# Three transformer layers on one core: a norm's scale deferred behind squared-ReLU layers, earlier row maxima in the sparse heads, and a reordered opening and convolution

## Chip, core and metric

The kernel runs on one core of a Trainium2 chip. The metric is device time in microseconds for one execution. The engines are TensorE (PE in the profile, with PEld for its weight loads), VectorE (DVE), ScalarE (ACT), GpSimd (POOL) and SyncE (SP, which here only issues DMAs). Each engine runs its own instructions in order and waits on semaphores.

## What is computed

One sequence of 256 tokens with 1024 features, float32, passes through three layers. Cut to what matters:

```python
for i in range(2):                      # first_block
    h = rms_norm(x, g[0])
    m = parallel_conv_mla(h, ...) if i == 0 else conformer_conv(h, ...)
    x = x + rms_norm(m, g[1])
    h = rms_norm(x, g[2])
    x = x + rms_norm(square(relu(h @ w1)) @ w2, g[3])
# third layer: differential attention (4 heads) + sparse attention (8 heads), then a gated FFN
h = rms_norm(x, pre);  x = x + rms_norm(hybrid_mixer(h), post)
h = rms_norm(x, pre2); x = x + rms_norm((silu(h @ w_gate) * (h @ w_up)) @ w_down, post2)

def rms_norm(x, g): return x * rsqrt(mean(x * x) + 1e-6) * g
def conformer_conv(h):                  # layer 1's mixer
    a, b = split(h @ w_pw1 + b_pw1)
    u = depthwise_conv(a * sigmoid(b), w_dw) + b_dw       # 31 taps
    return silu(layer_norm(u)) @ w_pw2 + b_pw2
```

`parallel_conv_mla` (layer 0) projects h to gate_b, gate_c, xs and latents, computes gate_b * conv3(gate_c * xs), an 8-head attention with rotary parts, and multiplies both by w_out. In the sparse attention each of 8 heads has a selected and a windowed branch plus a branch over 15 compressed tokens; at 256 tokens the first two are causal over everything.

## The kernel before

The 256 tokens are two tiles (m = 0, 1) of 128 partitions. All products are made to float32 accuracy from two-part numbers: a matrix W is kept as w_hi (rounded) and w_lo (the rest), activations as act_hl with a high half and a low half, and a product is high times high, high times low and low times high. Weights stream in pieces of 128x2048 values (1 MB) through a ring of four slots (three in the last stage). For each piece SP issues the load into `raw` (`load`), waiting for `w_split` of the piece that had the slot; POOL (`hi`, L575, in loops L590 and L685) or ACT (`hi`, L1338) writes w_hi; DVE (`lo`, L704, in halves `lo_half`, L718) writes w_lo and counts `w_split`; PE uses them and counts `pe_piece`.

PE has two kinds of product: `tall` puts activations as the stationary side, 128 tokens by up to 512 columns, into banks ACC to ACC+3; `wide` puts weights as the stationary side and leaves a transposed result in banks UP to UP+3, whose columns T to 2T (the product with the activations' low half) ACT copies out before DVE adds them. `wide_by_tile` does the first two pieces of a stage tile by tile: 32 high products of tile 0, 16 low products of tile 0 (`low_part`), then `turn_m` (eight transposes of tile 1's normalized rows), 32 high products of tile 1, and the remaining low products. `keep_warm` issues bf16 products with no use for the result.

A transition (`boundary(s, last)`, s = 1 to 5) lies between two products: post-norm of the result, addition to x, pre-norm, transposes. For a tile: ACT squares the result (`post_square`, L1342), POOL takes rstd (`row_rsqrt`, two steps L608, L609), DVE multiplies by the gain (`post_gain`, L749) and adds to x (`post_add`, L770), ACT squares the new x (`x_square`, L1342), POOL takes rstd again, DVE writes nrm (`pre_tile`, L780), PE transposes (L1727), ACT writes the high part (`high_tile`, L1366), DVE the low part (`low_tile`, L789). s = 1 leads into layer 0's squared ReLU, 2 into the convolution layer, 3 into layer 1's squared ReLU, 4 into the third layer, 5 into the last FFN. The opening is the second half of this alone, on x as loaded.

The order on each engine is written out by hand. Around the change it is:

- Opening: SP loads x0, x1 and four pieces; ACT asks for the first gain and the identity; POOL takes both rstd and then copies pieces; DVE does `pre_tile(0)`, `pre_tile(1)`, `low_tile(0)`, `lo_until(1)` (both first pieces), `low_tile(1)`.
- Projection: three wide products (gate_b, gate_c, xs) in the same banks. ACT copies four banks' second halves into ctmp (`wide_half`, L1414), DVE adds four banks (`wide_sum`, L878), and PE may then overwrite them (`wide_read`).
- First attention: DVE alternates `head_weigh(h)` and `head_max(h+2)`, with the low part of gate_b and two `lo_half` between heads; ACT has exponentials, copies of transposed probabilities and, at head 3, one `hi`.
- Convolution: per block b of 256 channels, PE has `pw` (in two halves), `forward(b)` (a DFT), `inverse(b)`; DVE has `gated`, `filtered`, `lo`. Then `row_stats`, normalization (L1066), `turn_normed`, SiLU (ACT L1550, L1554, L1328; DVE L1074, L736) and pw2.
- Sparse heads, u = 4 to 11: PE `scores_of(u)`, DVE `row_max(u)` (L1152, L1153), ACT `exponentials(u)` (L1630, four calls), DVE `weigh(u)` (L1162, L1173, L1177), PE `turn_of(u)` (six transposes), ACT `probs_turned(u)` (L1643), and for every pair of heads `out_of_pair` on PE. On DVE the compressed branch (`compressed_shift`, `compressed_weigh`) and the norm of the differential heads (L1244 to L1251) lie between.

```python
for t in range(DH + 2, HEADS + 2):      # DVE, the sparse loop's head
    if t <= HEADS:
        weigh(t - 1)
    if t < HEADS:
        row_max(t)
```

## Time and profile before

| | us |
|---|---|
| median of 3 timed runs (lowest to highest) | 965.57 (963.13 to 968.69) |
| profiled execution, its own time | 964.97 |
| its span, first to last instruction | 963.2 |
| PE busy | 912.3 (95%) |
| DVE busy | 690.8 (72%) |
| POOL busy | 290.2 (30%) |
| ACT busy | 260.5 (27%) |
| DMA, mean | 167 GB/s |

In the rows below a timeline line gives the start and the duration in us, the engine, the line of the kernel, the operation, what is written and read, and, in brackets, how long the engine was idle before it and who released it. Lines of equal instructions in a row are merged; "x2" is their number. "PEclk" is the clock granted to TensorE as a share of full speed.

### The profile page before, as it was taken

The numbers are of one execution on the slowest core, as the hardware profiler recorded it, in microseconds if no ns is written. First come the engines' busy times: TensorE is split into PE (matmuls) and PEld (weight loads), VectorE is DVE, ScalarE is ACT, GpSimd is POOL, SyncE is SP. The second block draws the span as 40 slices with busy tenths as digits, with TensorE's granted clock in tenths as the row PEclk, the third lists the DMA queues.
The fourth block names the chain that finished last, engine by engine and source line by source line (L and its number), as shares of the span: only waits on it lengthen the run. The fifth ranks groups of instructions, "written<-read, shape, count | busy, mean of one in ns | idle before, by whom it ended". The sixth has DMA issues, their size and how long they took to land.

```text
span 963.2 us, 12984 instructions
## 1 busy us (share of the span) xinstructions
PE 912.3 (95%) x4940; PEld 765.9 (80%) x4940; DVE 690.8 (72%) x695; ACT 260.5 (27%) x514; POOL 290.2 (30%) x176
## 2 busy tenths in 40 slices
PE   4999899999999999899999999999987999999996
PEld 4987688888888688688888888788855888888885
DVE  5668768876777645659877677677767578676774
ACT  2437441111112500323111111255665221111112
POOL 5000024444445332123344442400000234333331
PEclk9999999999999999999999999999999999999999
DMA  8752326555566354315555555456400437656631
GB/s 295 258 198 92 131 88 219 183 208 205 188 254 206 111 175 150 112 45 197 196 181 209 206 215 181 147 180 214 153 1 20 156 128 223 213 178 186 206 131 44
DMA packets 82437, 160.89 MB, mean 167 GB/s; under 512 B 4942, under 2 KB 40633, under 8 KB 82400
## 3 DMA queue, kind: packets, MB, share of 16 engines
q1 hardware_dynamic: 82112, 159.78, 48.3%
q8 instruction: 26, 0.43, 0.2%
q10 hardware_dynamic: 288, 0.59, 0.2%
q14 instruction: 11, 0.09, 0.0%
HBM read 159.31 MB, written 1.05 MB: 166 GB/s over the span
## 4 chain that ended last, share of the span: by engine, by line
PE 80%; DVE 11%; ACT 4%; POOL 2%; issue 2%; DMA 1%; DVEq 0%; SPq 0%; POOLq 0%; ACTq 0%
PE ps L1723 78%; DVE w_lo L704 2%; PE ps L1727 2%; ACT arena L1342 2%; ACT arena L1630 1%; DVE x_res L770 1%; DVE nrm L780 1%; POOL st L609 1%; POOL st L608 1%; DMA x_res<-in_x 1%; DVE arena L1177 1%; DVE w_lo L718 0%; DVE act_hl L789 0%; DVE st L1153 0%; DVE nrm L749 0%
## 5 line engine op out<-in xcount | busy, mean ns | idle before, releaser
L704 DVE TENSOR_TENSOR w_lo<-raw,w_hi 128x2048 fp32r<-128x2048 f32 (+3 forms) x140 | 331.5, 2394 | 35.3 <-POOL w_hi L685 21.7
L1723 PE MATMUL ps<-act_hl,w_hi 128*128 128x512 f32 (+1 forms) x1088 | 243.9, 371 | 9.5 <-DVE act_hl L789 7.6
L1723 PEld LDWEIGHTS ps<-act_hl,w_hi 128*128 128x128 f32 x1088 | 185.6, 194 | 39.7 <-DVE act_hl L789 9.0
L1723 PE MATMUL ps<-w_hi,act_hl 128*128 128x512 f32 (+3 forms) x656 | 184.3, 381 | 6.6 <-DVE act_hl L736 2.4
L590 POOL TENSOR_SCALAR w_hi<-raw 128x2048 fp32r<-128x2048 f32 x56 | 137.9, 2463 | 169.6 <-PE ps L1723 169.6
L1723 PE MATMUL ps<-w_hi,hl 128*128 128x512 f32 (+2 forms) x680 | 186.3, 384 | 0.6 <-DVE w_lo L704 0.6
L1723 PEld LDWEIGHTS ps<-w_hi,hl 128*128 128x128 f32 (+1 forms) x680 | 125.7, 189 | 24.1 <-issue 0.8
L1723 PEld LDWEIGHTS ps<-w_hi,act_hl 128*128 128x128 f32 x656 | 118.6, 188 | 31.6 <-DVE act_hl L736 2.9
L1723 PEld LDWEIGHTS ps<-act_hl,w_lo 128*128 128x128 f32 x1024 | 135.9, 190 | 8.3 <-DVE w_lo L704 0.2
L1723 PE MATMUL ps<-act_hl,w_lo 128*128 128x256 f32 (+1 forms) x1024 | 139.2, 281 | 0.0
L575 POOL TENSOR_SCALAR w_hi<-raw 128x2048 fp32r<-128x2048 f32 (+3 forms) x28 | 56.6, 2026 | 173.2 <-PE ps L1723 129.3
L1723 PE MATMUL ps<-w_lo,hl 128*128 128x512 f32 (+1 forms) x356 | 108.1, 378 | 0.0
L1723 PE MATMUL ps<-w_lo,act_hl 128*128 128x512 f32 (+1 forms) x328 | 107.4, 378 | 0.0
L685 POOL TENSOR_SCALAR w_hi<-raw 128x2048 fp32r<-128x2048 f32 x27 | 55.4, 2053 | 97.2 <-PE ps L1723 93.0
L1723 PEld LDWEIGHTS ps<-w_lo,hl 128*128 128x128 f32 (+1 forms) x356 | 65.3, 184 | 12.7
L1338 ACT ACTIVATE w_hi<-raw 128x2048 fp32r<-128x2048 f32 (+2 forms) x34 | 63.8, 1875 | 35.8 <-PE ps L1723 15.1
L998 DVE TENSOR_TENSOR hl<-arena,hl 128x512 fp32r<-128x512 f32 x28 | 53.7, 1923 | 25.3 <-ACT hl L1507 25.3
L1723 PEld LDWEIGHTS ps<-w_lo,act_hl 128*128 128x128 f32 x328 | 59.8, 188 | 11.0
L1499 ACT ACTIVATE arena<-ps 128x512 f32<-128x512 f32 x32 | 19.2, 598 | 143.4 <-PE ps L1723 143.4
L990 DVE TENSOR_TENSOR arena<-ps,arena 128x512 f32<-128x512 f32 x32 | 22.1, 690 | 43.7 <-ACT arena L1499 43.7
L1507 ACT ACTIVATE hl<-arena 128x512 fp32r<-128x512 f32 x28 | 17.8, 635 | 119.6 <-PE ps L1723 116.5
L1723 PE MATMUL ps<-arena 128*64 128x256 f32 (+6 forms) x288 | 43.2, 357 | 1.1 <-DVE arena L1043 0.9
(185 smaller groups left out, 709.2 us busy)
## 6 DMA issues: line engine op xcount, KB each, us to landing
raw<-in_mlp_w SPq DMA_DIRECT2D x64, 1024.0 KB, 5.2
raw<-in_w_gate SPq DMA_DIRECT2D x22, 512.0 KB, 4.0
raw<-in_w_up SPq DMA_DIRECT2D x22, 512.0 KB, 4.9
raw<-in_w_down SPq DMA_DIRECT2D x11, 1024.0 KB, 4.9
raw<-in_odd_w_pw SPq DMA_DIRECT2D x16, 512.0 KB, 4.9
raw<-in_w_in SPq DMA_DIRECT2D x8, 1024.0 KB, 5.4
raw<-in_even_w_in SPq DMA_DIRECT2D x6, 1024.0 KB, 8.1
raw<-in_even_w_out SPq DMA_DIRECT2D x4, 1024.0 KB, 6.0
```

The source lines that it names most:

```text
L575: gp.tensor_scalar(w_hi[slot_of(n)][:, 0:w], raw[slot_of(n)][:, 0:w], 1.0, 0.0, ALU.mult, ALU.add).then_inc(S("w_hi"), 1)
L590: gp.tensor_scalar(w_hi[slot_of(n)][:, :], raw[slot_of(n)][:, :], 1.0, 0.0, ALU.mult, ALU.add).then_inc(S("w_hi"), 1)
L685: gp.tensor_scalar(w_hi[slot_of(q)][:, :], raw[slot_of(q)][:, :], 1.0, 0.0, ALU.mult, ALU.add).then_inc(S("w_hi"), 1)
L704: tt(w_lo[slot_of(n)][:, 0:w], raw[slot_of(n)][:, 0:w], w_hi[slot_of(n)][:, 0:w].bitcast(F32), ALU.subtract).then_inc(S("w_split"), 1)
L990: link(tt(htmp[:, c, :], ps[:, UP + 2 * j:UP + 2 * j + 2, 0:T], htmp[:, c, :], ALU.add))
L998: tt(dst[:, c, T:2 * T], hb[:, c, :], dst[:, c, 0:T].bitcast(F32), ALU.subtract)\
L1338: f(w_hi[slot_of(n)][:, 0:w], raw[slot_of(n)][:, 0:w], ACT.Copy).then_inc(S("w_hi"), 1)
L1342: f(junk[:, m, at:at + src.shape[1]], src, ACT.Square, scale=1.0 / D ** 0.5, accum_out=total)\
L1499: f(htmp[:, 2 * j:2 * j + 2, :], ps[:, UP + 2 * j:UP + 2 * j + 2, T:2 * T], ACT.Copy)\
L1507: f(dst[:, 2 * j:2 * j + 2, 0:T], hb[:, 2 * j:2 * j + 2, :], ACT.Copy).then_inc(S("hid_hi"), 1)
L1723: return pe.matmul(o, l, r, start=start, stop=stop, skip_group_check=True)
L1727: return pe.transpose(o, src, ident[0:src.shape[0], 0:src.shape[0]])
```

## The change

Four things, on the same products with the same operands.

1. In transitions 1 and 3 (`SCALE_LATER`) the pre-norm does not wait for the rstd of the new x. `post_add_pre` multiplies by whatever rs_pre holds, c, from the norm before. Since the squared-ReLU layer is homogeneous of degree two, its result comes out (c/r)^2 times too large, r being the right scale, and the post-norm behind it removes any factor except in its eps. POOL's `next_eps` computes the eps that makes it exact, EPS * (c*c*(mean x^2 + EPS))^2, for use in transition s + 1. ACT writes tile 1's high part before it squares x. On PE, `wide_by_tile` has tile 1's transposes ahead of tile 0's low products (`turn_late=False`), here and in the opening.
2. Sparse heads: PE issues the scores one head further ahead and DVE takes the maximum of the next head before it weighs the current one.
3. Opening: loads in the order x0, piece 0, x1, piece 1; the first gain is asked for when x0 has landed; DVE has `low_tile(0)` and the low part of piece 0 before tile 1's norm.
4. Smaller orders: projection copies and sums in halves; first attention with the gate product earlier and weight work behind the heads; w_out's piece 0 with its w_lo products last; `inverse` one block behind; layer norm written by halves; SiLU's high part before the next tanh; `lo_half` before `pre_tile(1)` in transitions 2 and 5; w_lo of the last piece before the last SiLU; four `keep_warm` products after tile 1's transposes in transitions 4 and 5. TILE_STEP = (4, 4) names the grouping of the copies and leaves it as it was.

```diff
@@ SP @@
                 for m in range(M):
                     sp.dma_start(x[:, m, :], a["x"][0, m * P:(m + 1) * P, :]).then_inc(S(f"x_in{m}"), 16)
-                for n in range(4):
+                    load(m)
+                for n in range(2, 4):
                     load(n)
@@ POOL @@
+                def next_eps(m):
+                    squares[0] += 2
+                    gp.wait_ge(S("ssq"), squares[0])
+                    h, c = ssx[:, 2 * m:2 * m + 1], rs_pre[:, m:m + 1]
+                    me.link(gp.tensor_scalar(h, h, ssx[:, 2 * m + 1:2 * m + 2], EPS, ALU.add, ALU.add))
+                    me.link(gp.tensor_tensor(h, h, c, ALU.mult))
+                    me.link(gp.tensor_tensor(h, h, c, ALU.mult))
+                    me.link(gp.tensor_scalar(eps_next[:, m:m + 1], h, h, EPS, ALU.mult, ALU.mult))
...
                 row_rsqrt(rs_pre, ssx, 0)
+                hi_until(0)
                 row_rsqrt(rs_pre, ssx, 1)
@@ DVE @@
+                def post_add_pre(s, m, g):
+                    next_rstd()
+                    ssqs[0] += 4
...
+                    for i, h in enumerate(half):
+                        stt(x[:, m, h], nrm[:, m, h], rs_post[:, m:m + 1], x[:, m, h], ALU.mult, ALU.add)\
+                            .then_inc(S("x_new"), 1)
+                        dve.wait_ge(S("x_new"), 4 * (s - 1) + 2 * m + i + 1)
+                        stt(nrm[:, m, h], x[:, m, h], rs_pre[:, m:m + 1], gain[g % 4][:, h], ALU.mult, ALU.mult)\
+                            .then_inc(S("normed"), 1)
...
                 pre_tile(0, 0)
+                low_tile(0, ACC)
+                lo_until(0)
                 pre_tile(1, 0)
-                low_tile(0, ACC)
                 lo_until(1)
                 low_tile(1, ACC)
...
                 row_max(DH)
                 compressed_kv()
+                row_max(DH + 1)
                 weigh(DH)
-                row_max(DH + 1)
                 compressed_shift()
-                compressed_weigh()
                 for t in range(DH + 2, HEADS + 2):
-                    if t <= HEADS:
+                    if t < HEADS and t != DH + 3:
+                        row_max(t)
+                    if t <= HEADS and t != DH + 3:
                         weigh(t - 1)
-                    if t < HEADS:
-                        row_max(t)
                     if t == DH + 2:
+                        compressed_weigh()
+                        row_max(DH + 3)
+                        weigh(DH + 2)
...
-                lo_until(N_PIECES - 2)
+                lo_until(N_PIECES - 1)
                 silu_gate(FF_BLOCKS - 1)
                 ff_lo(FF_BLOCKS - 1, act_hl)
-                lo_until(N_PIECES)
@@ ACT @@
+                small(cst[:, 0:P], a["shape_constants"][:, 0:P], "cst_in")
+                act.wait_ge(S("x_in0"), 16)
                 small(gain[0][:, :], a["sandwich_gains"][0, 0, :].partition_broadcast(P), "gain0")
-                small(cst[:, 0:P], a["shape_constants"][:, 0:P], "cst_in")
...
-                    if h == 3:
-                        hi(c + 10)
...
                 pair_out(2, "pv", 4, 6)
+                hi(c + 10)
...
                     if k % 2:
+                        if k > 1:
+                            silu_high(k // 2 - 1)
                         act.wait_ge(S("z"), k + 1)
@@ PE @@
-                        if m == 1:
+                        if m == 1 and turn_late:
                             turn_m(turn_bank, 1)
+                            keep_warm(turn_bank, 4)
...
                         if m == 0:
+                            if not turn_late:
+                                turn_m(turn_bank, 1)
                             arrived(n)
                             low_part(n, slice(0, P), range(4))
...
-                    inverse(b)
+                    if b:
+                        inverse(b - 1)
+                inverse(3)
...
+                scores_of(DH + 2)
                 turn_of(DH)
                 for t in range(DH + 2, DH + NH + 1):
-                    if t < DH + NH:
-                        scores_of(t)
+                    if t + 1 < DH + NH:
+                        scores_of(t + 1)
```

## Rows read from the trace of the kernel before

**Rows 1.** The page, part 1: busy time, share and instructions of each engine.

```profile
PE 912.3 (95%) x4940; PEld 765.9 (80%) x4940; DVE 690.8 (72%) x695; ACT 260.5 (27%) x514; POOL 290.2 (30%) x176
```

**Rows 2.** Windows: length, busy us of each engine, PEclk, DMA share, GB/s.

```profile
0.00:27.00 27.00, 13.52 (x87) 12.91 (x88) 13.51 (x10) 6.23 (x13) 14.25 (x13) 1.00 0.87 306
...
84.00:110.00 26.00, 21.62 (x131) 14.82 (x130) 22.57 (x49) 19.72 (x53) 0.00 (x0) 1.00 0.13 41
...
138.00:152.00 14.00, 12.14 (x87) 11.31 (x87) 10.75 (x10) 5.99 (x6) 2.99 (x4) 0.88 0.48 174
152.00:315.00 163.00, 163.00 (x823) 139.01 (x823) 127.28 (x79) 22.73 (x42) 76.21 (x33) 1.00 0.58 205
...
388.00:404.00 16.00, 12.39 (x62) 8.52 (x61) 10.75 (x16) 5.49 (x11) 1.57 (x4) 1.00 0.41 131
...
431.00:443.00 12.00, 10.14 (x82) 9.31 (x81) 10.76 (x10) 5.91 (x6) 0.65 (x2) 1.00 0.44 155
...
688.00:742.00 54.00, 42.78 (x351) 31.11 (x351) 39.80 (x111) 36.55 (x115) 1.95 (x2) 0.97 0.09 30
```

**Rows 3.** DMA issues in 0 to 40 us: queue, size, us to landing.

```profile
gain<-in_sandwich_gains ACTq DMA_DIRECT2D x1, 512.0 KB, 5.6
```

**Rows 4.** Timeline of the opening.

```profile
10.69 1.89 POOL L575 TENSOR_SCALAR w_hi<-raw 128x2048 fp32r<-128x2048 f32 x1
10.74 3.04 DVE L780 SCALAR_TENSOR_TENSOR nrm<-x_res,st,gain 128x512 f32<-128x512 f32 x2 [0.77 <-POOL st L609]
...
14.44 6.13 PE L1723 MATMUL ps<-act_hl,w_hi 128*128 128x256 f32 x32 [3.04 <-DVE act_hl L789]
14.91 6.64 DVE L704 TENSOR_TENSOR w_lo<-raw,w_hi 128x2048 fp32r<-128x2048 f32 x2
...
15.78 7.52 POOL L575 TENSOR_SCALAR w_hi<-raw 128x2016 fp32r<-128x2016 f32 x2 [0.23 <-DMA raw<-in_even_w_in]
...
24.19 4.09 PE L1723 MATMUL ps<-act_hl,w_hi 128*128 128x256 f32 x32 [0.98 <-DVE act_hl L789]
```

**Rows 5.** Timeline of tile 1 in transition 1, and the same products in transition 3.

```profile
135.79 1.41 DVE L770 SCALAR_TENSOR_TENSOR x_res<-nrm,st,x_res 128x512 f32<-128x512 f32 x2 [0.42 <-POOL st L609]
...
139.04 1.42 DVE L780 SCALAR_TENSOR_TENSOR nrm<-x_res,st,gain 128x512 f32<-128x512 f32 x2 [1.83 <-POOL st L609]
...
142.37 5.42 PE L1723 MATMUL ps<-act_hl,w_hi 128*128 128x256 f32 x32 [1.20 <-DVE act_hl L789]
...
434.79 4.10 PE L1723 MATMUL ps<-act_hl,w_hi 128*128 128x256 f32 x32 [1.20 <-DVE act_hl L789]
```

**Rows 6.** Timeline, first products of the third projection.

```profile
60.64 2.12 PE L1723 MATMUL ps<-act_hl,w_hi 128*128 128x512 f32 x8 [1.28 <-DVE arena L878]
```

**Rows 7.** Timeline of the first attention: ACT's weight copy, and w_out's first products.

```profile
96.50 1.92 ACT L1338 ACTIVATE w_hi<-raw 128x2048 fp32r<-128x2048 f32 x1
...
109.38 0.72 PE L1723 MATMUL ps<-w_hi,act_hl 128*128 128x512 f32 x2 [0.69 <-ACT arena L1460]
```

**Rows 8.** Timeline, end of the convolution: last inverse, first products of pw2.

```profile
390.53 3.72 PE L1723 MATMUL ps<-arena 128*128 128x256 f32 x16 [0.95 <-DVE arena L1043]
...
403.05 0.74 PE L1723 MATMUL ps<-w_hi,act_hl 128*128 128x512 f32 x2 [2.44 <-DVE act_hl L736]
```

**Rows 9.** Timeline of the sparse heads, and w_out_2's first products.

```profile
712.69 1.54 PE L1727 MATMUL ps<-cst,arena 128*128 128x128 f32 x6 [2.77 <-DVE arena L1177]
...
732.45 0.37 ACT L1630 ACTIVATE arena<-ps,st 128x128 f32<-128x128 f32 x1 [1.72 <-DVE st L1153]
...
734.61 1.01 DVE L1177 TENSOR_SCALAR arena<-arena,st 128x128 f32<-128x128 f32 x4
...
736.58 0.37 ACT L1630 ACTIVATE arena<-ps,st 128x128 f32<-128x128 f32 x1 [1.44 <-DVE st L1153]
...
741.33 0.73 PE L1723 MATMUL ps<-w_hi,act_hl 128*128 128x512 f32 x2 [0.65 <-DVE act_hl L734]
```

**Rows 10.** Timeline, the last piece's first products.

```profile
950.94 0.70 PE L1723 MATMUL ps<-w_hi,act_hl 128*128 128x512 f32 x2 [0.96 <-DVE w_lo L704]
```

More of the change, by code:

```diff
@@ L623, in boundary @@
                         bias_low(0, bias_pw1)
-                    row_rsqrt(rs_post, ssh, 0)
-                    all_normed = 4 + 4 * s + (2 if s >= 3 else 0)
-                    row_rsqrt(rs_pre, ssx, 0)
+                    eps = [eps_next[:, m:m + 1] if s - 1 in SCALE_LATER else EPS for m in range(M)]
+                    row_rsqrt(rs_post, ssh, 0, eps[0])
+                    all_normed = 4 + 4 * s + (4 if s >= 3 else 0)
+                    if s in SCALE_LATER:
+                        next_eps(0)
+                    else:
+                        row_rsqrt(rs_pre, ssx, 0)
                     gp.wait_ge(S("normed"), all_normed - 2)
@@ L1380, in boundary @@
                         x_square(1, h)
-                    high_tile(1, TURN_BANK[s])
+                    if s not in SCALE_LATER:
+                        high_tile(1, TURN_BANK[s])
                     if s != 4:
@@ L1771, in wide, with tall @@
                     ins.then_inc(S("pe_piece"), 1)
-                def tall(n, bank, lhs, lhs_k0, first, last, k, cols, turn_=0, per=0, tiles=range(M), free=True, half=None, apart=2, split=512):
-                    arrived(n, turn_, per)
+                def tall(n, bank, lhs, lhs_k0, first, last, k, cols, turn_=0, per=0, tiles=range(M), free=True, half=None, apart=2, split=512, low_last=False):
+                    if low_last:
+                        pe.wait_ge(S("w_hi"), n + 1)
+                    else:
+                        arrived(n, turn_, per)
```

205 lines of the change are left out of this document (117 added, 88 removed).

## Prediction

> **What bounds the kernel now.** TensorE. It is busy 912.3 of 963.2 us [rows 1], so I read the profile in this order: the page for that share, a table of windows for where the missing 51 us lie, the list of who waits for whom for the releasers, and then the timeline around each hole. In the table the reader is to see that the long stages have no hole at all (163.00 busy of 163 in the first squared-ReLU block), while 13.5 us are missing in the opening, 4.4 in the first attention, 1.9 in each of the two transitions into a squared-ReLU layer, 3.6 at the end of the convolution, 11.2 in the sparse heads [rows 2]. What the change can give is in these holes, plus two stretches at half clock: the granted clock is 0.88 on average in 138 to 152 and 0.97 in 688 to 742, and 1.00 elsewhere in the table. Nothing else is priced: the change leaves every matrix product as it is.
>
> The profiled execution took 964.97 us with a span of 963.2; the median of the three timed runs is 965.57. The sum is made against 964.97, and I carry it over unchanged, since the 0.6 us between them is less than the spread of the runs.
>
> **Opening (+1.5 us).** The loads go x0, w0, x1, w1; the first gain is asked for on ACT's queue only once x0 has landed. Before, that gain took 5.6 us from issue to landing [rows 3] while x0 and x1 shared the engines. Issued at about 4.9 (x0 now travels nearly alone; before, both were under way from 0.7) and given a somewhat better rate than in the ramp, it lands near 9.6, and the first norm cannot start before. Bounds: 8.7 if it needs 3.8 us, 11.7 if x0 comes no earlier than now and the 5.6 stand. Meanwhile POOL copies w0 as soon as it is there, 1.89 us [rows 4]. The trace shows what happens when DVE's norm meets such a copy: the pair of multiplications takes 3.04 us at 10.74, against 1.42 with POOL idle [rows 4, 5]. Two DVE subtractions of w_lo take 6.64 instead of 4.6, and the two POOL copies beside them 7.52 instead of 3.8: the engines take turns, one instruction each [rows 4]. So the order in which they ask counts. Followed: copy w0 to 10.5, first half norm 11.2, transposes, ACT, low part, first real product at 13.7 instead of 14.44. Then alternately copy w1 to 15.2, low part of w0 to 17.5, copy w2 to 19.3, norm of tile 1 first half to 20.0, copy w3 to 21.9, second half to 22.6, low part of w1 to 24.9, low part of tile 1 to 25.6. The second tile's products then start at 25.7, where they start at 24.19 now [rows 4]. The order by which x1's norm stood ahead of the first low part is what the change gives up. Bounds: -2.0 if the turns fall so that DVE is never refused, +3 if the gain lands at 11.7 and the idle keeps the clock low.
>
> The Trainium skill, in "SBUF — State Buffer", section on who interferes with whom, says that a DVE instruction with two SBUF inputs and a GpSimd instruction that reads SBUF lock each other out for the whole instruction. The durations in [rows 4] agree; without the rule, and with the durations just split, one would book the opening as a gain of 2 us. The Trainium skill, in "DMA: Bandwidth & Descriptors", section on queues and rings, has the DMA engines serve the queues in turn, packet by packet; by it the gain gets half the rate and lands near 9.6. No row of before shows ACT's queue against a full SP queue.
>
> **Projection halves (-0.9).** The product after gate_c waits 1.28 us for one ACT copy and one DVE addition over four banks [rows 6]. Split in two, each half costs some 0.6 and 0.7 instead of 1.0 and 1.2, and PE needs only the first. Bounds 0 and -1.3.
>
> **First attention (-1.3).** ACT's copy of the last w_out piece, 1.92 us, stands between two heads [rows 7] and goes behind them; so do 1.2 us of gate low part and 2.4 of w_lo on DVE. Walking the eight heads by engine order (PE about 1.1 for scores, 0.6 for transposes, 1.1 per pair for values; ACT 0.95 and 0.6; DVE 0.7 and 0.8) PE becomes the fuller one but still waits for the last pairs; w_out starts at 108.1 instead of 109.38 [rows 7]. The work taken out is late next: w_lo of w_out's pieces. Piece 0 now runs its high parts first (16 products of 0.23, 3.6 us), and the low part is written before they end. The bound is the whole hole, -4.4; the other 0.
>
> **Transition into layer 0's squared ReLU (-2.5).** Now: post-norm's rstd of tile 1 at 135.79, x written, squares on ACT, two POOL steps, pre-norm at 139.04 after 1.83 idle, transposes, products at 142.37 after another 1.20 [rows 5]. The change multiplies by the scale left over from the norm before, at once: four DVE instructions from 135.79 end at 138.7, so the transposes end at 139.3 (after some 0.5 of new waiting for the second half), the sixteen low products of tile 0, which stood before them, now fill the copies' time (1.9 us), and the products start at 141.2: -1.2. The 32 products took 5.42 us at half clock here and 4.10 in the same place of the other layer [rows 5]; without the long wait I expect 4.1: -1.3. Its chance is less than certain, since the other layer has the same wait at full clock. The squares and next_eps move behind; POOL has nothing else until the next copy, and what they feed is a whole layer away. The correction itself costs eight tiny POOL instructions per layer.
>
> **The same in layer 1 (-1.2),** by the same steps: products at 434.79 after 1.20 idle [rows 5] start at 433.6. Bounds for either: 0 and -1.9.
>
> **Convolution (-2.0).** The last inverse transform waits 0.95 us for the filter [rows 8]; with the previous inverse behind the last forward one, that is covered, and row statistics fit in before it ends. Normalizing by halves brings the transposes forward by 1.2, but ten and four warming products stand before them, so only 0.4 arrives. SiLU's high part ahead of the next tanh saves another 0.6 of the 2.44 us wait [rows 8]. Bounds -0.9 and -3.4.
>
> **Sparse heads (-3.2).** Between one head's exponentials and the next lie 4.13 us (732.45 to 736.58), in which ACT works 1.6 and then waits while DVE weighs (1.4) and only then takes the maximum (1.0) [rows 9]. With scores one head ahead and the maximum first, the exponentials no longer wait for the weighing; late next is PE, 3.3 us a head (scores 1.3, transposes 0.9, half a pair 1.1). In the first four heads DVE also has the compressed branch and the norm of the differential heads, about 1.2 us per head, and ACT still has its 1.9 us weight copies in between. Walked by order of the queues, exponentials of the seventh head and later start 1 to 4 us earlier and w_out_2 starts at 738.1 instead of 741.33 [rows 9]. This includes the half clock that followed the 2.77 us wait [rows 9]. Bounds: 0 (a wait for the compressed branch takes the place) and -8, what is left of the 11.2 us hole and the low clock if only the waits ahead of the head loop stay [rows 2].
>
> **The end (-0.9).** The last low part, ahead of the last SiLU, fills DVE's idle and removes a 0.96 us wait [rows 10]. The copy it needs is there before. **Warming products** (four of 0.22) added where tile 1's transposes are done lie inside waits of about 1 us: 0, at worst +0.3 at each of two places.
>
> Sum: 1.5 - 0.9 - 1.3 - 2.5 - 1.2 - 2.0 - 3.2 - 0.9 = -10.5, so 954.5 us.
>
> **Rivals.** (a) The opening gains 2.0: 951.0. For it: the total work on the two engines is unchanged. Against: the 3.04 and 7.52 us. (b) The sparse heads gain nothing, because the DVE extras and ACT's weight copies still set the pace: 957.7. For it: DVE is the busiest beside PE there. (c) Clock: other waits draw a low stretch; each costs about 1.3 us, and before had two. With three in after, 4.0 worse than booked: 958.5. (d) Slower: the gain's load starves. If ACT's queue gets nothing while SP's is full, the gain lands with SP's first lull at about 22 us, and the second tile's products start 12 us after it, 34: the opening costs 9.8 and the total is 962.8. If it lands only behind the three gains that SP asks for next, about 30, the cost is 17.8 and the total 970.8. The loss outweighs the gain from a landing of 24.6 on. Against it: the gain of before landed in 5.6 us beside two loads of SP. (e) The deferred scale does not remove the wait, because the second half of the pre-norm arrives as late: 957 to 958.
>
> **How the numbers follow.** Forecast 0.52 (951 to 957), (a) 0.15, (b) 0.12, (c) 0.08, (e) 0.07, (d) 0.04 at 962.8 and 0.02 at 970.8. Measurement tells about 0.5% (4.8 us) from no change. Up to 960.7 is faster: all but (d) and a small tail of (c) and (e), 0.89; within 0.5% 0.08; slower 0.03. The range 947 to 960 reaches from (a) with a fuller attention and sparse gain to (c).
>
> **What would show it.** Right: windows over 84 to 110 with 1 us less idle; products after the two transitions behind a wait under 0.3 us, with the squares on ACT after the transposed copies; exponentials under 3.5 us apart; no wait for w_lo at the end; in the opening a DVE norm stretched beside a POOL copy. Wrong: a first product before 13 us and the second tile's before 23, a wait for the maximum as long as before, or a half-clock stretch in a long stage. My largest doubts are the opening's sign and the sparse size.

## The result, and the profile after

| | before | after |
|---|---|---|
| median of the timed runs, us | 965.68 (963.13 to 968.69) | 955.73 (954.66 to 956.50) |
| ratio, 95% interval | | 0.990 (0.987 to 0.993) |
| profiled execution: time and span, us | 964.97, 963.2 | 956.50, 954.4 |
| TensorE busy, us | 912.3 | 914.3 |

The change is 1.0% faster; forecast were 954.5 us and a range of 947 to 960. TensorE is still the bound, and its busy time has even grown, though its products are the same but for eight warming ones.
```profile
PE 914.3 (96%) x4948; PEld 767.9 (80%) x4948; DVE 691.4 (72%) x700; ACT 259.9 (27%) x517; POOL 299.2 (31%) x184
```

Windows over the same stages as in [rows 2], each shifted by what the kernel had gained by then (columns: window, length, busy us of each engine with instructions, granted clock, DMA share, GB/s):

```profile
0.00:27.00 27.00, 12.74 (x77) 11.84 (x78) 12.47 (x10) 6.35 (x13) 11.19 (x13) 1.00 0.87 306
84.00:109.00 25.00, 21.53 (x133) 15.34 (x131) 20.14 (x47) 18.18 (x53) 0.00 (x0) 1.00 0.00 1
135.00:149.00 14.00, 13.07 (x105) 12.43 (x105) 12.72 (x14) 7.86 (x11) 8.56 (x6) 1.00 0.40 149
320.00:333.00 13.00, 11.76 (x36) 7.51 (x35) 8.67 (x8) 6.76 (x6) 3.76 (x3) 0.74 0.49 153
385.00:401.00 16.00, 14.53 (x74) 11.04 (x73) 12.18 (x18) 4.57 (x10) 1.57 (x4) 1.00 0.42 131
427.00:439.00 12.00, 11.07 (x92) 10.54 (x91) 10.79 (x11) 7.60 (x11) 6.81 (x5) 1.00 0.43 144
684.00:735.00 51.00, 43.27 (x352) 31.43 (x353) 39.97 (x110) 36.09 (x115) 1.86 (x2) 0.97 0.08 31
```

The reader is to see two things. The holes have shrunk where the change works: 25.00 - 21.53 = 3.5 us are missing in the attention (4.4 before), 0.9 in either transition into a squared-ReLU layer (1.9 before), 1.5 at the end of the convolution (3.6), 7.7 in the sparse heads (11.2). In the opening the hole is 14.3 (13.5). And a window that [rows 2] did not need to show, the transition out of the first squared-ReLU layer, now runs at a mean clock of 0.74: 13 x 0.26 x 2 = 6.8 us of it at half clock. The lengths of low stretches below are worked out from windows in the same way.

For the sum I cut both traces at the same products. The cut M1 is the start of the second tile's products in the opening, M2 of w_out's, M3 the first tile's transposes into the transition behind the first squared-ReLU layer, M4 the first products of pw2, M5 and M6 two products at 608 and 697, M7 w_out_2's first, M8 one at 787. Each is a row of the timeline. Transitions 1 to 3 are those into the first squared-ReLU layer, out of it into the convolution layer, and into the second squared-ReLU layer. Times in us:

| stretch | before | after | difference | forecast | what changes in it |
|---|---|---|---|---|---|
| start to M1 | 24.19 | 25.49 | +1.30 | +1.5 | opening |
| M1 to M2 | 85.19 | 82.83 | -2.36 | -2.2 | projection halves, first attention |
| M2 to M3 | 207.35 | 204.77 | -2.58 | -2.5 | transition 1 |
| M3 to M4 | 86.32 | 87.20 | +0.88 | -2.0 | transition 2, convolution |
| M4 to M5 | 209.39 | 207.78 | -1.61 | -1.2 | transition 3 |
| M5 to M6 | 89.27 | 89.34 | +0.07 | 0 | |
| M6 to M7 | 39.62 | 36.47 | -3.15 | -3.2 | sparse heads |
| M7 to M8 | 53.42 | 53.29 | -0.13 | 0 | |
| M8 to the end | 168.45 | 167.23 | -1.22 | -0.9 | low part of the last piece |
| span | 963.2 | 954.4 | -8.8 | -10.5 | |

Eight stretches out of nine are within 0.5 us of their terms. The one that is not is M3 to M4, by 2.9 us, and the experiments begin there. (The medians differ by 9.9, the two profiled spans by 8.8; the runs of after alone spread over 1.8.)

The opening (timeline; columns: start, duration, engine, line, operation, idle before and its releaser), and the gain's row among the DMA issues (the last number is us from issue to landing):

```profile
8.92 1.90 POOL L585 TENSOR_SCALAR w_hi<-raw 128x2048 fp32r<-128x2048 f32 x1
...
12.07 1.42 DVE L808 SCALAR_TENSOR_TENSOR nrm<-x_res,st,gain 128x512 f32<-128x512 f32 x2 [12.07 <-DMA gain<-in_sandwich_gains]
...
13.11 2.14 POOL L585 TENSOR_SCALAR w_hi<-raw 128x2048 fp32r<-128x2048 f32 x1 [1.24 <-DMA raw<-in_even_w_in]
...
15.56 6.24 PE L1776 MATMUL ps<-act_hl,w_hi 128*128 128x256 f32 x32 [0.65 <-DVE act_hl L831]
15.58 1.89 POOL L585 TENSOR_SCALAR w_hi<-raw 128x2016 fp32r<-128x2016 f32 x1 [0.34 <-DMA raw<-in_even_w_in]
...
16.19 3.42 DVE L732 TENSOR_TENSOR w_lo<-raw,w_hi 128x2048 fp32r<-128x2048 f32 x1
18.10 3.25 POOL L585 TENSOR_SCALAR w_hi<-raw 128x2016 fp32r<-128x2016 f32 x1 [0.63 <-DMA raw<-in_even_w_in]
...
19.53 3.01 DVE L808 SCALAR_TENSOR_TENSOR nrm<-x_res,st,gain 128x512 f32<-128x512 f32 x2
...
25.49 4.06 PE L1776 MATMUL ps<-act_hl,w_hi 128*128 128x256 f32 x32 [0.50 <-DVE act_hl L831]
```

```profile
gain<-in_sandwich_gains ACTq DMA_DIRECT2D x1, 512.0 KB, 7.2
```

The first norm starts 2.5 us later than forecast and runs free of POOL's copy (1.42 for the pair), since that copy was over by then; the second tile's norm takes 3.01 beside a later copy (18.10), as the pair did in [rows 4].

Both transitions into a squared-ReLU layer, second tile (timeline):

```profile
134.46 0.75 DVE L818 SCALAR_TENSOR_TENSOR x_res<-nrm,st,x_res 128x512 f32<-128x512 f32 x1 [0.41 <-POOL st L619]
...
135.25 0.75 DVE L821 SCALAR_TENSOR_TENSOR nrm<-x_res,st,gain 128x512 f32<-128x512 f32 x1
...
137.51 0.66 PE L1780 MATMUL ps<-cst,nrm 128*128 128x128 f32 x4 [0.63 <-DVE nrm L821]
...
139.74 4.04 PE L1776 MATMUL ps<-act_hl,w_hi 128*128 128x256 f32 x32
...
142.04 2.16 POOL L628 TENSOR_TENSOR st<-st 128x1 f32<-128x1 f32 x1
...
428.16 0.65 PE L1780 MATMUL ps<-cst,nrm 128*128 128x128 f32 x4 [0.63 <-DVE nrm L821]
```

The pre-norm starts 0.79 us behind the start of the x update, where it stood 3.25 behind in [rows 5]. The 32 products start without a wait and take 4.04 instead of 5.42. The four transposes of the second half wait 0.63, in both layers.

The sparse heads (timeline): two exponentials of the last heads, and the waits around them.

```profile
719.40 0.93 PE L1776 MATMUL ps<-arena 64*128 64x128 f32 x8 [1.65 <-ACT arena L1683]
...
721.71 2.41 PE L1776 MATMUL ps<-arena 128*64 128x256 f32 x16
...
725.67 0.36 ACT L1683 ACTIVATE arena<-ps,st 128x128 f32<-128x128 f32 x1
...
728.21 0.41 ACT L1683 ACTIVATE arena<-ps,st 128x128 f32<-128x128 f32 x1
...
733.88 0.72 PE L1776 MATMUL ps<-w_hi,act_hl 128*128 128x512 f32 x2 [1.15 <-DVE act_hl L762]
```

The exponentials of the last four heads (from 717.64, 720.18, 725.67 and 728.21) come in pairs, 2.5 us apart within a pair and 5.5 between the pairs, where [rows 9] has 4.13; those of the first four are 3.6, 6.2 and 4.1 apart. So the last three gaps together are 10.6 us against 12.5 before. The longest wait is 1.65 instead of 2.77. The sixteen products at 721.71, most of them at half clock, take 2.41 us; the same sixteen at 728.62 take 1.47.

### The profile page after: what moved, and what is told of

Read it like the earlier page. It is cut to its first block, busy times and chain, and to the rows that moved or that the text cites. A ratio compares the mean times of both kernels' runs of the same rounds, so it can differ in the third digit from the quotient of the medians.

```text
span 954.4 us, 13013 instructions
## 1 busy us (share of the span) xinstructions
PE 914.3 (96%) x4948; PEld 767.9 (80%) x4948; DVE 691.4 (72%) x700; ACT 259.9 (27%) x517; POOL 299.2 (31%) x184
## 4 chain that ended last, share of the span: by engine, by line
PE 81%; DVE 10%; ACT 4%; issue 2%; POOL 2%; DMA 1%; DVEq 0%; POOLq 0%; ACTq 0%
PE ps L1776 79%; DVE w_lo L732 3%; PE ps L1780 2%; ACT arena L1390 1%; POOL st L618 1%; DVE x_res L798 1%; DMA gain<-in_sandwich_gains 1%; POOL st L619 1%; DVE nrm L808 1%; ACT w_hi L1386 1%; ACT arena L1683 0%; DMA x_res<-in_x 0%; DVE nrm L777 0%; DVE nrm L821 0%; POOL w_hi L585 0%
## 5 line engine op out<-in xcount | busy, mean ns | idle before, releaser
L585 POOL TENSOR_SCALAR w_hi<-raw 128x2048 fp32r<-128x2048 f32 (+3 forms) x28 | 54.4, 1944 | 170.0 <-PE ps L1776 138.1
```

Source lines behind the costliest of these rows:

```text
L585: gp.tensor_scalar(w_hi[slot_of(n)][:, 0:w], raw[slot_of(n)][:, 0:w], 1.0, 0.0, ALU.mult, ALU.add).then_inc(S("w_hi"), 1)
```

## The experiments

All of them are edits of the changed kernel. "Undone" means the lines of before, with one exception, said at e3_no_defer. Their medians are of four runs; since low-clock stretches come and go from trace to trace, the verdicts rest on the cuts M1 to M8, not on the medians.

### e1_warm_t2: what took the 2.9 us between M3 and M4

```
                     if m == 1:
+                        keep_warm(ACC, 5)
                         turn_m(ACC, 1)
                         pe.wait_ge(S("dft_in"), 16 * 16)
                         filter_of(0)
+                        keep_warm(ACC, 3)
```

> The changed kernel with eight warming products more at the transition out of the first squared-ReLU layer: five ahead of the second tile's transposes, where TensorE waits 1.23 us in the changed kernel (322.02), and three behind the filter's products. Theory: that wait, 0.29 us longer than the 0.94 at the same place of the kernel before, is what cost the clock (granted 0.62 over 325 to 333, where the sixteen products took 6.27 us against 3.93 before). With the wait filled the clock stays at 1.00, the sixteen products take about 3.9 us, and the kernel takes 955.7 - 3.4 + 0.3 = 952.6 us. Rival: the clock falls for what lies longer before (the whole stage has run faster) or falls later instead; then the time is 955.7 to 956.2, with the low stretch there or in the next stage.

Measured: 953.13 us (952.51 to 955.28), ratio 0.990 (0.989 to 0.992), span 950.4. The same two windows of after and of this kernel:

```profile
320.00:325.00 5.00, 3.76 (x15) 1.93 (x14) 3.37 (x6) 2.22 (x3) 1.01 (x2) 0.93 0.00 0
325.00:332.00 7.00, 7.00 (x18) 4.75 (x17) 5.30 (x3) 4.54 (x4) 2.21 (x1) 0.56 0.75 232
```

```profile
320.00:325.00 5.00, 4.86 (x22) 2.53 (x21) 3.37 (x6) 2.15 (x5) 1.01 (x2) 1.00 0.00 0
325.00:332.00 7.00, 7.00 (x31) 5.17 (x30) 5.67 (x4) 4.92 (x4) 1.83 (x1) 1.00 0.54 166
```

In 325 to 332 TensorE is busy all the time in both, but gets through 18 matmuls in the one and 31, three of them warming ones, in the other. With the wait filled the clock stays up, and M3 to M4 takes 84.53 instead of 87.20: 2.7 us. The low stretch is what took the time, as the theory has it. What I had not expected is that the one in the sparse heads went too (M6 to M7 34.88 instead of 36.47), though nothing was changed there.

Why the wait is longer than before can be read from the second tile's rows of this transition, in before (first line) and in after:

```profile
323.57 0.30 POOL L608 TENSOR_SCALAR st<-st 128x1 f32<-128x1 f32 x1 [2.37 <-ACT arena L1342]
```

```profile
319.08 1.22 DVE L746 TENSOR_TENSOR w_lo<-raw,w_hi 128x1024 fp32r<-128x1024 f32 x1
...
320.02 0.45 POOL L618 TENSOR_SCALAR st<-st 128x1 f32<-128x1 f32 x1 [2.37 <-ACT arena L1390]
```

The change itself put the half low part (`lo_half`) ahead of the second tile's pre-norm here, and POOL's step beside it takes 0.45 instead of 0.30. From the x update to the pre-norm pass 3.46 us (317.75 to 321.21) instead of 3.25; the remaining 0.08 of the 0.29 lies ahead of the x update. That the length of the wait decides is not shown. The six traces with this wait unfilled fit it, though: 0.94 and 1.14 us with no low stretch (before, e3_no_defer), 1.21 to 1.24 with one (after, e2_open_old, e4_sparse_old, e11_warm_sparse), each in one trace.

### e2_open_old: the opening undone

Loads in the order x0, x1, w0 to w3; the gain asked for ahead of everything on ACT's queue; x1's norm ahead of the first low parts; the second tile's transposes late.

> The changed kernel with the opening of the kernel before: loads x0, x1 ahead of the four weight pieces, the gain asked for at once, x1's norm ahead of the first low parts on POOL and DVE, the second tile's transposes behind the first tile's low products. Theory: the second tile's products start at 24.2 again instead of 25.5, the time falls by 1.3 to 954.4, if the low-clock stretch at the transition out of the first squared-ReLU layer stays; 951.0 if it goes. Rival (the opening of the change is a gain that shows only later, because DVE and POOL have then done more of the work): the product behind gate_c, 36 us later, starts as late as or later than in the changed kernel (60.95), and the time is 955.7 or more.

Measured: 955.20 us (954.62 to 955.63), span 953.3, 1.1 less than after. The two rows that answer to those of after:

```profile
10.80 3.05 DVE L806 SCALAR_TENSOR_TENSOR nrm<-x_res,st,gain 128x512 f32<-128x512 f32 x2 [0.78 <-POOL st L618]
...
24.46 4.06 PE L1772 MATMUL ps<-act_hl,w_hi 128*128 128x256 f32 x32 [1.07 <-DVE act_hl L829]
```

The second tile's products start at 24.46; with the opening of the change they start between 25.30 and 26.00 in the eight traces that have it unchanged, with the old one at 24.19, 24.46 and 24.70 in three (before, this run, e9_warm_open_old). M1 to M2 stays at 82.83, so nothing is given back later: the opening of the change costs 0.6 to 1.8 us, 1.0 in this pair. The rival falls.

### e3_no_defer: the deferred scale undone

```
-        SCALE_LATER = (1, 3)
+        SCALE_LATER = ()
```

> The changed kernel without the deferred scale: in all transitions the second tile's pre-norm waits for its own row sums (four warming products stand behind its transposes). Theory: the second tile's products start 1.2 us later at both transitions, and the 32 of the first take 5.4 us at the lower clock again or 4.1 with the warming products; 955.7 + 2.4 + (0 to 1.3) = 958.1 to 959.4, or 3.4 less if the low stretch at the next transition goes. Rival: the wait that the deferral removes is hidden elsewhere (the added second-half wait of 0.63 us, low parts of the weights late): 956.5 at most, with the w_lo pieces of the next products as the late ones.

Measured: 955.61 us (955.50 to 957.21), span 953.9: no slower than after. In one thing this kernel is not the one before: in transitions 1 and 3 it has the half low part ahead of the second tile's pre-norm, and four warming products behind the transposes. By the total the rival would win. By the cuts it does not: M2 to M3 is 205.87 (+1.10) and M4 to M5 209.58 (+1.80), so taking the deferral out costs 2.9 us, more than my 2.4; and M3 to M4 is 83.92 (-3.28), because no low stretch came at the second transition. Transition 1 in this kernel:

```profile
138.90 1.32 PE L1780 MATMUL ps<-cst,nrm 128*128 128x128 f32 x8 [0.57 <-DVE nrm L808]
...
140.05 1.03 PE L1776 MATMUL ps<-mask_neg,mask_id 128*128 128x512 bf16 x4
...
141.06 4.07 PE L1776 MATMUL ps<-act_hl,w_hi 128*128 128x256 f32 x32
```

The 32 products take 4.07 us here too. So the 1.3 us of half clock that before pays in this place [rows 5] does not hang on the deferral: with about the old wait, partly filled by four warming products, it is gone as well. Of the 1.80 in transition 3, 0.7 comes ahead of the second tile's pre-norm: its x is updated 25.50 us after M4 instead of 24.82, behind 0.79 us of waiting for POOL instead of 0.41.

### e4_sparse_old: the sparse heads undone

The weights of a head again come ahead of the next head's maxima, and the scores are one head ahead only.

> The changed kernel with the sparse heads in the order of the kernel before: weights of a head ahead of the next head's maxima, scores one head ahead only. Theory: 3.2 us more, 958.9, with the exponentials of the last heads 4.1 us apart again where they are 2.5 to 5.5 apart in pairs now, and the last wait ahead of w_out_2's products as before. Rival: the gain of the sparse stage came from elsewhere (work of the stages before done earlier by DVE and ACT): then under 1 us more, 955.7 to 956.7.

Measured: 957.19 us (956.16 to 958.12), span 955.8, 1.4 more than after; between theory and rival. Waits of TensorE in this kernel:

```profile
708.06 0.88 PE L1778 MATMUL ps<-cst,arena 128*128 128x128 f32 x6 [2.77 <-DVE arena L1223]
...
735.38 0.73 PE L1774 MATMUL ps<-w_hi,act_hl 128*128 128x512 f32 x2 [0.65 <-DVE act_hl L762]
```

The wait of 2.77 is back exactly as in [rows 9], but the six transposes behind it take 0.88 us and not 1.54: this run drew no low stretch in the sparse heads (it did at transition 2). Its M6 to M7 is 38.30. Against e1_warm_t2, the run of the new order without a stretch (34.88), the order is worth 3.4 us; before (39.62) against after (36.47), both with one, 3.2. The theory holds at equal clock, and my sentence that the 3.2 "includes the half clock that followed the 2.77 us wait" falls: after had a stretch as well, further on in the stage (2.41 instead of 1.47 us at 721.71).

### e5_attn_old, e6_conv_old, e7_halves_end_old: three more parts undone

These three start from e1_warm_t2, so that no stretch at transition 2 blurs them. e5 puts ACT's copy and DVE's low parts of w_out back among the heads; e6 restores `inverse(b)` behind `forward(b)`, normalization by tile and tanh ahead of the SiLU copy; e7 restores four-bank copies and sums in the projection and the last low part behind the last SiLU.

> The changed kernel with the warming of e1_warm_t2 (953.1 us, no low-clock stretch), and the first attention's tail in the order of the kernel before: ACT's copy of the last output-weight piece between two heads, gate and low parts among the heads on DVE, the first piece's products in one pass. Theory: the output products start 1.37 us later than in e1_warm_t2 (108.72), at 110.1; 954.5 us if no clock stretch is drawn, 956.0 to 957.9 with one. Rival (w_lo of those pieces, late next, had taken part of it back, or the attention's gain came from the projection halves ahead of it): under 0.5 us later.

> The changed kernel with the warming of e1_warm_t2, and the convolution in the order of the kernel before (inverse transform right behind its own block's forward transform, normalization by tile, tanh ahead of the SiLU high part). My sum booked 2.0 us for it; the two traces with their low stretch taken off show nearer 2.5. Theory: 953.1 + 2.5 = 955.6 us, with a wait of about 0.95 ahead of the last inverse transform and 2.4 ahead of the products behind it (403.05 in the kernel before), without a low stretch. Rival: one of the three edits does nothing and the stage loses only the 1.2 us by which that last wait shrank: 954.3.

> The changed kernel with the warming of e1_warm_t2, and both small edits undone, far apart from each other: the projection's copies and sums over four banks in one piece (start), and the last low part behind the last SiLU (end). Theory: the product after gate_c waits 1.28 us again instead of 0.33 (0.95 more), and the products of the last piece wait 0.96 again: 953.1 + 1.9 = 955.0 us. Rival: the wait of 0.96 at the end was the order's own and costs nothing of the span, as the last products wait for the down-projection's hidden rows anyway: 954.1.

Measured: 956.09, 957.35 and 957.34 us; spans 953.3, 954.2 and 955.7. One row, two rows and two rows of their timelines, in this order:

```profile
109.61 0.73 PE L1777 MATMUL ps<-w_hi,act_hl 128*128 128x512 f32 x2 [0.69 <-ACT arena L1514]
```

```profile
387.61 3.72 PE L1779 MATMUL ps<-arena 128*128 128x256 f32 x16 [0.95 <-DVE arena L1092]
...
400.13 0.74 PE L1779 MATMUL ps<-w_hi,act_hl 128*128 128x512 f32 x2 [2.44 <-DVE act_hl L764]
```

```profile
62.43 2.12 PE L1777 MATMUL ps<-act_hl,w_hi 128*128 128x512 f32 x8 [1.28 <-DVE arena L929]
...
943.46 0.70 PE L1777 MATMUL ps<-w_hi,act_hl 128*128 128x512 f32 x2 [0.96 <-DVE w_lo L732]
```

Against e1_warm_t2, M1 to M2 grows by 1.31 in e5 (attention) and by 1.02 in e7 (halves), M3 to M4 by 2.66 in e6, M8 to the end by 1.25 in e7. The waits of [rows 6, 8, 10] come back to the hundredth. The forecasts for those parts were 1.3, 0.9, 2.0 and 0.9, and the rivals of all three kernels fall. Their medians are 1.6 to 2.3 us above what was expected, by the low-clock stretches that each of them drew in the sparse heads: M6 to M7 is 36.45, 36.46 and, with a stretch of 6.8 us, 37.81, where e1_warm_t2 has 34.88 by the same instructions.

### e8_gain_now and e10_open_mixed: what sets the second tile's start

Both have the warming products of e1_warm_t2, and on ACT's queue:

```
+                small(gain[0][:, :], a["sandwich_gains"][0, 0, :].partition_broadcast(P), "gain0")
                 small(cst[:, 0:P], a["shape_constants"][:, 0:P], "cst_in")
-                act.wait_ge(S("x_in0"), 16)
-                small(gain[0][:, :], a["sandwich_gains"][0, 0, :].partition_broadcast(P), "gain0")
```

and in e10 besides, on DVE:

```
                 low_tile(0, ACC)
-                lo_until(0)
                 pre_tile(1, 0)
-                lo_until(1)
+                lo_until(0)
                 low_tile(1, ACC)
+                lo_until(1)
```

> The changed kernel with the warming of e1_warm_t2, and the first gain asked for at once instead of behind x0's landing; the rest of the opening stays. Theory (the gain's 7.2 us behind x0 are what the opening pays): the first norm starts at about 9.0 instead of 12.1, beside POOL's copy of w0, the first product at 13.0 to 14.0 instead of 15.6, the second tile's at about 24.5 instead of 25.9; 951.9 us. Rival (the alternation of POOL's copies and DVE's low parts, and the landing of w1 at 13.1, set the second tile's start): the first product comes earlier, the second tile's at 25.5 or later, and the time stays at 952.7 to 953.1.

> As e8_gain_now, with another order on DVE in the opening: norm and low part of the first tile, norm of the second tile, low part of w0, low part of the second tile, low part of w1. Theory (what sets the second tile's start is which DVE instructions stand ahead of it, each stretched by a copy on POOL): the norm of the second tile is through by 16.7 instead of 21.8, its low part by 23, and its products start at 22.9 instead of 24.76; 951.2 us. Rival (the first tile's low products, which wait for w_lo of w0, are late next and then w_lo of w1 holds the products behind the second tile's): the second tile's products start at 24 or later, or a wait for w_lo of over 1 us stands behind them; 952.7 us.

Measured: e8 953.09 us (951.35 to 955.70), span 949.2; e10 951.77 us (950.81 to 953.83), ratio 0.987 (0.985 to 0.989). In e8 the first product starts at 13.17, 2.4 earlier than in after, but only 0.7 of it reaches the second tile (1.1 against e1_warm_t2); the timeline shows why:

```profile
17.20 4.61 DVE L808 SCALAR_TENSOR_TENSOR nrm<-x_res,st,gain 128x512 f32<-128x512 f32 x2
...
24.76 4.07 PE L1775 MATMUL ps<-act_hl,w_hi 128*128 128x256 f32 x32 [0.50 <-DVE act_hl L831]
```

The second tile's norm now meets two POOL copies and takes 4.61 us for 1.42 of work. In e10 it goes ahead of w_lo of w0:

```profile
13.59 2.81 DVE L808 SCALAR_TENSOR_TENSOR nrm<-x_res,st,gain 128x512 f32<-128x512 f32 x2
...
16.32 3.94 DVE L732 TENSOR_TENSOR w_lo<-raw,w_hi 128x2048 fp32r<-128x2048 f32 x1
...
22.16 4.05 PE L1775 MATMUL ps<-act_hl,w_hi 128*128 128x256 f32 x32
...
48.04 1.22 PE L1775 MATMUL ps<-act_hl,w_lo 128*128 128x256 f32 x8 [0.71 <-DVE w_lo L732]
```

The products start at 22.16 without any wait, 2 us earlier than in the kernel before. By M2 1.4 of it is given back, half of that in the wait for w_lo at 48.04, as e10's rival has it in a smaller size: e10 reaches M2 at 106.41, e8 at 107.60, e1_warm_t2 at 108.72. (In e12_all, with the same opening, that wait is 0.17 and only 0.4 is given back.) The medians show less of this than the spans, 949.2 in e8 against 950.4 in e1, and e10's 951.4 holds two low stretches in the sparse heads (M6 to M7 38.14). The theories hold for what sets the second tile's start. The Trainium skill, "SBUF — State Buffer", section on who interferes with whom, says that contention over the port pair that DVE and GpSimd share is an exclusive lock. The 4.61, 2.81 and 3.94 agree.

### e9_warm_open_old: do two gains add up

> The warming of e1_warm_t2 together with the opening of the kernel before, as in e2_open_old. Theory: the two add up, 24.2 to 24.5 for the second tile's products against 25.9, no low-clock stretch at the second transition: a span of 949.0 to 949.4 and 951.7 us. Rival (a low-clock stretch comes by where a stage happens to lie in time, and the sparse stage now starts 1.4 us earlier than in e1_warm_t2): a stretch in the sparse heads, whose stage takes 36.5 instead of 34.9 us, and 953.3 us.

Measured: 953.04 us (952.87 to 953.98), span 950.8. M3 to M4 is 84.56, as the theory has it, and M1 24.70, 0.2 later than its range; but the sparse heads drew a stretch (M6 to M7 36.45), which is the rival's time. Its window over the beginning of the heads:

```profile
694.00:703.00 9.00, 8.85 (x75) 6.03 (x76) 5.03 (x16) 4.74 (x20) 0.00 (x0) 0.81 0.01 2
```

The rival's reason does not hold as it stands: e8_gain_now reaches M6 at 693.91 and e9 at 693.90, with the same code from there on, and one draws a stretch and the other none.

### e11_warm_sparse: the waits in the sparse heads filled

```
+                keep_warm(UP + 2, 2)
                 turn_of(DH)
   ...
+                    if t == DH + 5:
+                        keep_warm(UP + 3, 6)
                     if t + 1 < DH + NH:
                         scores_of(t + 1)
+                    if t == DH + 3:
+                        keep_warm(UP + 2, 4)
```

> The changed kernel (without the warming of e1_warm_t2) with twelve warming products more in the sparse heads, inside the three waits of 0.61, 1.06 and 1.65 us at 707.41, 712.34 and 719.40. Theory (those waits draw the low stretch of 720 to 724): the stretch goes, w_out_2's products start 36.47 - 1.6 = 34.9 us after the transposes at 697.41, as in e1_warm_t2; 954.2 us. Rival (the products stand in the way of the real ones, 0.22 us each for a part of them): no stretch but 0.6 to 1.2 us of it given back, 955.0; or the stretch stays and the time is 956.3.

Measured: 953.18 us (951.81 to 956.48), span 951.0. The heads, and the wait that was 1.65:

```profile
696.00:731.00 35.00, 30.50 (x258) 20.14 (x257) 29.48 (x88) 27.66 (x84) 1.86 (x2) 1.00 0.01 1
```

```profile
717.65 0.93 PE L1776 MATMUL ps<-arena 64*128 64x128 f32 x8 [0.42 <-ACT arena L1683]
```

M6 to M7 takes 34.96: no stretch, and the twelve products cost 0.08 us. At the second transition, left as in after, a stretch of 3.4 us came instead of 6.8 (M3 to M4 85.53).

### e12_all: everything together

The opening of e10_open_mixed with both sets of warming products.

> The opening of e10_open_mixed, the warming at the second transition of e1_warm_t2 and the twelve warming products in the sparse heads of e11_warm_sparse, all in one kernel. Theory (with the two places warm no low-clock stretch is drawn wherever the stages lie in time): granted clock 1.00 throughout, 34.9 to 35.0 us for the sparse heads, a span of 951.4 - 3.4 = 948.0 us, since e10_open_mixed had two low stretches of 1.6 and 1.8 us in its sparse heads; 950.0 us, ratio 0.985 to 0.987. Rival (what draws a stretch is the run of half-filled work ahead of those waits too, and its place in time decides): a low stretch earlier in the sparse stage, 949.6 of span and 951.7 us, no better than e10_open_mixed.

Measured: 950.05 us (949.49 to 951.70), ratio to before 0.986 (0.983 to 0.989), span 947.3. It is ahead of both kernels. Windows over the opening, transition 2 and the sparse heads:

```profile
0.00:27.00 27.00, 15.36 (x102) 14.58 (x103) 13.55 (x12) 6.00 (x13) 12.16 (x13) 1.00 0.86 296
325.00:332.00 7.00, 7.00 (x27) 4.62 (x26) 3.47 (x5) 2.99 (x5) 4.99 (x3) 1.00 1.05 349
692.00:727.00 35.00, 30.52 (x258) 20.20 (x258) 29.47 (x89) 27.63 (x84) 1.86 (x2) 1.00 0.01 1
```

No low clock is recorded in any of them, and TensorE is busy for 15.36 us of the opening's 27 where [rows 2] has 13.52. The theory holds for this execution. That no run of this kernel draws a stretch is not shown: the spans of the four are 947.3, 947.9, 948.0 and 949.5, and the mean clock of the last is 0.997 against 0.998 and 0.999.

## Why the prediction was right, and where not

**The bound and the places.** All the gain came out of the holes that were named, and TensorE stayed the bound.

**Opening (+1.5, measured +1.3, undone 1.0).** Sign and size were right, the size by luck; the path was not. The landing of the gain, 9.6 in the forecast, came at 12.0: 7.2 us after its issue, longer than the 5.6 of [rows 3] and later than my upper bound of 11.7. I had given the gain a somewhat better rate than in the ramp, without a row for it; instead it was under way together with w0 and x1, and its 512 KB took longer. The late norm then fell behind POOL's first copy instead of beside it, and the first product came 1.9 us late (15.56, forecast 13.7). But while DVE was late, POOL went on: besides w1's copy, over at 15.25 as in my walk, it had the next piece's over at 17.47 (15.58 and 1.89), which the walk put between the low part of w0 and the second tile's norm. So that low part ended 2.1 us late (19.61, forecast 17.5), but the norm behind it met one copy and not two, and ended at 22.54 (forecast 22.6). Two errors of about 2 us cancelled. e8 and e10 show that the step that I called decisive, who asks first, DVE or POOL, is indeed what sets the second tile's start: three orders give 24.46, 24.76 and 22.16.

**Projection halves and first attention (-0.9 and -1.3, undone 1.02 and 1.31).** Right as worked out. In the attention the last wait ahead of w_out's products is unchanged, 0.69; what moved was everything before it.

**Transition 1 (-2.5, measured -2.6).** The start of the products moved by 1.6 (booked 1.2) and they took 1.4 less (booked 1.3); 0.4 was lost again behind them. The clock half of the term was right in size and wrongly attributed: e3 has neither the deferral nor the low stretch. By e3 the deferral is worth 1.1 here and up to 1.8 in the other layer (booked 1.2, measured 1.6), some 0.2 of it for e3's half low part ahead of the pre-norm (0.2 at transition 2).

**Convolution (-2.0, undone 2.7).** Mis-sized. The waits of 0.95 and 2.44 us were read from [rows 8] correctly. But I booked 0.6 of the second wait for the SiLU's order and 0.4 for the normalization by halves, and the wait shrank by 1.24, to 1.20; the three edits together gave another 0.5 us beyond the two waits' 2.2. Which of them gave how much is not shown, since e6 undoes all three.

**Sparse heads (-3.2, measured -3.2, order alone 3.4).** Right in size; the part of the reason that spoke of the clock was wrong, as e4 shows. The sign that I had named, exponentials "under 3.5 us apart", did not come: they are 2.5 and 5.5 apart by turns in the last four heads, 3.5 on average (4.15 before). From the first head's exponentials to the last's pass 29.8 us instead of 33.9, and 0.9 of these 4.1 is lost again between the last exponentials and w_out_2's products.

**The end (-0.9, undone 1.25), warming products (0).** Right in the main. Twelve products more in waits cost 0.08 (e11), and eight of which three were not in one about 0.6 (M3 to M4 of e1 against e3, which also differ in the deferral).

**The step that failed: transition 2, which has no term in the sum.** "Nothing else is priced", the prediction says, though the change reorders DVE there; only rival (c) covers it, at 1.3 us per stretch. The half low part ahead of the pre-norm made POOL's step slower, the wait ahead of the second tile's transposes went from 0.94 to 1.23 us, the clock fell for 6.8 us behind it, and M3 to M4 paid 2.7 to 3.3 us (e1, e3). Whether the 0.3 us drew the stretch is open. With the stretch taken out, the sum gives a span of 963.2 - 8.8 - 3.0 = 951.4, against a forecast of 952.7: the other parts were 1.3 us better than booked. That the median still came out only 1.2 us above the forecast is partly luck, a missed loss set against gains booked too low.

**Rivals.** (a) fell: the opening gained nothing. (b) fell by e4. (c) came in its mechanism: the stretch at transition 1 went, one at transition 2 came, twice as long, and the sparse heads had one, a cost of 4.3 to 4.9 us in this trace where (c) has 4.0. Its time of 958.5 did not come, because the other parts gained more. (d) fell: the gain landed in 7.2 us beside a full queue. (The landing at which its loss outweighs the gain is 24.2 by its own terms, not 24.6; nothing hangs on it.) (e) fell by the cuts of e3, though by the medians alone (955.61 against 955.73) one would have believed it.

## What to carry over

Compare two kernels cut by cut at the same instruction, not by their totals: here the undone deferral and the changed kernel take the same time, and each of its two parts, 2.9 us lost and 3.3 us of clock won, shows only in the cuts. Price every place whose order a change touches, even where it seems to cost nothing: a half low part of 1.22 us moved ahead of a norm made up most of the growth of a wait from 0.94 us to 1.23, and a low stretch of 6.8 us stood behind it. A few warming products inside the waits of about 1 us that are left on TensorE are cheap: twelve of them cost 0.08 us. Where DVE and POOL both work out of SBUF, write down who asks first for each pair of instructions; moving one norm of 1.4 us ahead of one low part of 2.3 brought the next tile forward by 2.6 us.

## What was not expected of the hardware

The low clock comes and goes by itself. The sparse heads' new order ran from the cut M6 on with the same instructions in ten traces without warming there: eight drew low stretches (six of 3.4 us, one of 6.8, one of two times 3.4) and two none, and two of them that reach M6 within 0.01 us of each other differ. The old order drew one in before and none in e4, with the same wait of 2.77 us. A stretch of 3.4 us costs 1.3 to 1.6 us, one of 6.8 costs 2.7 to 3.3. The Trainium skill, "TensorE: Matmul & The Clock Gate", section on the HAM clock gate, says that the number of slow matmuls at one kernel's start differs from run to run; the low stretches in these traces do so in the middle of a kernel. The four runs of one kernel differ in the same way: those of e8_gain_now have spans of 949.2 and 949.5 us at a mean clock of 0.999, 952.4 at 0.996 and 953.6 at 0.994. What decides between a stretch and none stays open; where the waits were filled, none came, at transition 2 in eight traces and in the sparse heads in two.

The recorded clock does not explain the opening. There the 32 products of the first tile take 6.24 us and those of the second 4.06, 16 products against 27 in the windows 16 to 19 and 26 to 29, and the profile gives the clock as 1.00 in both. What slows the first ones is not shown; a 1.00 in the window of an opening should not be taken for full speed.

The arithmetic on single columns is cheap only while DVE leaves POOL alone: the correction's four steps on 128x1 take 0.30, 0.19, 0.19 and 0.27 us for the first tile (from 129.18), and 0.71, 1.06, 2.16 and 2.19 for the second (from 140.12), beside DVE's low parts of weights. No cost of it shows in M2 to M3.
